# Twenty-one of the twenty-four unread matmuls in each of five RMSNorm waits are taken out of a two-layer diffusion backbone

## The chip, the cores and the metric

The kernel runs on one core of one Trainium2 chip. The metric is the device time of one execution in microseconds (us). A core has TensorE (matmuls), VectorE, ScalarE, GpSimd, and SyncE, which here issues DMAs.

## The reference

The program runs two layers over 256 latent tokens and 256 context tokens of width 1024, in fp32. Every layer is a half-step SwiGLU feed-forward, a token mixer (layer 0: a convolution module beside windowed attention; layer 1: a two-directional mLSTM), and a second half-step feed-forward. Each of these sub-layers begins with an RMSNorm, modulated by a conditioning vector, and the last layer is followed by one more.

```python
def rmsnorm(x, g):
    xf = x.astype(jnp.float32)
    y = xf * lax.rsqrt(jnp.mean(xf * xf, axis=-1, keepdims=True) + EPS)
    return (y * g.astype(jnp.float32)).astype(x.dtype)

def ffn_half(x, mods, g, w_gu, w_d):
    shift, scale, gate = mods
    h = modulate(rmsnorm(x, g), shift, scale) @ w_gu
    hg, hu = jnp.split(h, 2, axis=-1)
    return x + 0.5 * gate * ((jax.nn.silu(hg) * hu) @ w_d)
```

## The kernel before

All state is kept with the model width on the partitions: xT holds 8 tiles (KT = 8) of 128 partitions by 512 columns, the tokens of both streams. Seven norms are numbered 0 to 6. Norm 0 opens the first feed-forward (f0), norm 1 the even mixer (ev_in), norm 2 the feed-forward f1, norm 3 f2, norm 4 the odd mixer (od_gate, od_in), norm 5 f3 and norm 6 the output. Norms 0 to 4 run over 512 columns, norms 5 and 6 over 256, the latent tokens alone.

Weights come in units of 128 by 2048 numbers. For each, SyncE loads raw, ScalarE rounds it to w_hi (L936), and VectorE takes the difference as w_lo (L1241). Every product is three matmuls: high by high, low by high and high by low (L467 to L469). The buffers of raw, w_hi and w_lo are double, so unit u + 2 can be made only when TensorE is done with unit u. Activations are split in the same way into hn_hi and hn_lo.

A norm n passes through four engines, each of which works through its own list in order. Semaphores tie the lists together:

- ScalarE squares the tiles of xT as they are finished (L974), VectorE adds seven of them into acc (L1255).
- TensorE, in norm(n), waits for the last square and the last addition, and sums acc and the last square over the partitions against a column of ones, into one column for each block of 128 tokens (L524, L525).
- ScalarE takes the root (L946), and then makes w_hi of the unit LATE_UNIT[n], which it had put off for the norm. VectorE inverts (L1280), spreads the result on a diagonal (L1281), and makes w_lo of the same late unit.
- TensorE broadcasts the diagonal over all partitions with one fp32 matmul (L530).
- VectorE scales a tile into t_ring (L1297), ScalarE adds the shift and rounds to hn_hi (L952), and VectorE makes hn_lo (L1304) and raises hn_made. After each of the first tiles the first products of the next stage can begin: first_units takes five tiles of two units in turns (two tiles at 256 columns), 12 products for each tile.

In norms 1 to 5 TensorE also runs matmuls whose result nobody reads. keep_busy(n, count) first waits until the unit u = LATE_UNIT[n] - 1 is made and its bank is free, and then issues count matmuls of w_hi by w_hi, 512 columns each, into that bank (L516). The first real product of the stage overwrites it. norm(n) calls it three times: ahead of the wait for the squares, between the sums and the wait for the diagonal, and behind the broadcast. The table BUSY holds the three counts, 6, 7 and 11. Norms 0 and 6 have none.

Of the kernel before, what the change touches and what calls it, by code (L numbers as in the profile page):

```python
# [86 lines left out]
def build(nc, t, out):  # L87
# [3 lines left out]
    with ExitStack() as ctx:  # L91
# [216 lines left out]

        LATE_UNIT = {1: U["ev_in"] + 1, 2: U["f1upA"] + 1, 3: U["f2upA"] + 1, 4: U["od_in"], 5: U["f3upA"] + 1, 6: NU}
        ADDS = KT - 2  # L310
        BUSY = {n: (6, 7, 11) for n in range(1, 6)}

        STEP_TILE = ((2, 3, 0, 1), (3, 2, 1, 0))

# [148 lines left out]
        def _(pe):  # L463
# [46 lines left out]
            def keep_busy(n, count):  # L510

                u = LATE_UNIT[n] - 1
                pe.wait_ge(lo_made, u + 1)
                pe.wait_ge(unit_evac, u - 1)
                for _ in range(count):
                    pe.matmul(ps[:, bank(u, 1), :], w_hi[:, u % 2, 0:P], w_hi[:, u % 2, 0:TOK], start=True, stop=True)  # L516

            def norm(n):
                if n in BUSY:
                    keep_busy(n, BUSY[n][0])  # L520
                pe.wait_ge(sq_added, ADDS * (n + 1))
                pe.wait_ge(sq_made, KT * (n + 1))
                for i in range(W[n] // P):
                    pe.matmul(ps[:, 6, i:i + 1], acc[:, i * P:(i + 1) * P], ones[:, 0:1], start=True, stop=False)  # L524
                    last = pe.matmul(ps[:, 6, i:i + 1], sq[:, 1, i * P:(i + 1) * P], ones[:, 0:1], start=False, stop=True)  # L525
                last.then_inc(norm_mm, 1)
                if n in BUSY:
                    keep_busy(n, BUSY[n][1])
                pe.wait_ge(rstd_made, n + 1)
                pe.matmul(ps[:, 7, 0:W[n]], ones, rstd[:, 0:W[n]], start=True, stop=True).then_inc(rstd_mm, 1)  # L530
                if n in BUSY:
                    keep_busy(n, BUSY[n][2])

# [1335 lines left out]
```

## Time and profile before

| | us |
|---|---|
| median of 3 runs | 1868.83 |
| lowest and highest run | 1868.31, 1869.6 |
| the profiled execution | 1873.79 |
| span of its trace | 1871.9 |

| engine | busy us | share of the span |
|---|---|---|
| TensorE, matmuls | 1768.6 | 94% |
| TensorE, weight loads | 1483.5 | 79% |
| VectorE | 1161.2 | 62% |
| ScalarE | 622.2 | 33% |
| GpSimd | 68.4 | 4% |

The times of instructions below are those of the profiled execution. Records of matmuls overlap: one of 512 columns lasts 0.39 us in the trace while the next starts 0.23 us after it. So the pace of TensorE is read from starts and not from durations. The granted clock (PEclk) is 1.00 at 2.4 GHz and 0.50 at 1.2 GHz; its mean over the profiled execution is 0.973. A wait shows as idle time ahead of an instruction, in brackets, with what ended it.

### The profile page before, as it was taken

The page shows a single profiled execution, that of the slowest core. Times are in us where ns is not written, and L with a number is a line of the kernel's source. Part 1 is how long each engine was busy: PE and PEld are TensorE (multiplying, and loading weights), DVE is VectorE, ACT ScalarE, POOL GpSimd, SP SyncE. Part 2 cuts the span into 40 slices and gives each one's busy share as a digit, 9 for nine tenths or more (in the row PEclk, how much of TensorE's full clock was granted, in tenths as well). Part 3 has the DMA queues.
Part 4 walks back from the last instruction along what each step waited for, and adds up shares of the span by engine and source line. Part 5 has one row for each costly group of instructions (what it writes and reads, how often), then busy time and mean ns, then how long its engine had stood idle before and what let it go on. Part 6 is the DMA issues. An engine that isn't in the chain of part 4 may idle for free.

```text
span 1871.9 us, 23296 instructions
## 1 busy us (share of the span) xinstructions
PE 1768.6 (94%) x9187; PEld 1483.5 (79%) x9187; DVE 1161.2 (62%) x1765; ACT 622.2 (33%) x824; POOL 68.4 (4%) x133
## 2 busy tenths in 40 slices
PE   6899999999876999999999999999999999899997
PEld 4688888877543778888888788888887999899996
DVE  4477667875869557776778577533335536665454
ACT  3322223233564442312322332222224323454442
POOL 0011001100000000100100000000000000000000
PEclk9899999999986999999999999999999999999998
DMA  8455556552100125554556254232231222234543
GB/s 326 162 186 180 185 170 194 171 192 88 46 23 23 54 71 170 184 182 173 192 171 199 90 173 162 91 113 90 79 103 68 88 71 91 91 134 170 192 163 107
DMA packets 49041, 253.36 MB, mean 135 GB/s; under 512 B 5569, under 2 KB 7105, under 8 KB 32577
## 3 DMA queue, kind: packets, MB, share of 16 engines
q1 hardware_dynamic: 30384, 184.10, 28.4%
q0 software_dynamic: 18576, 68.17, 11.4%
q8 instruction: 54, 0.88, 0.2%
q14 instruction: 27, 0.21, 0.0%
HBM read 251.20 MB, written 1.05 MB: 135 GB/s over the span
## 4 chain that ended last, share of the span: by engine, by line
PE 86%; DVE 8%; ACT 4%; issue 1%; DMA 1%; SPq 0%; ACTq 0%; DVEq 0%
PE ps L467 27%; PE ps L468 27%; PE ps L469 27%; DVE y L1441 2%; DVE w_lo L1241 2%; ACT w_hi L936 1%; PE ps L804 1%; DVE t_ring L1297 1%; PE ps L833 1%; DVE hn_lo L1304 1%; ACT hn_hi L952 0%; PE ps L676 0%; PE ps L830 0%; PE ps L690 0%; DMA xT<-in_xT 0%
## 5 line engine op out<-in xcount | busy, mean ns | idle before, releaser
L467 PE MATMUL ps<-hn_hi,w_hi 128*128 128x512 f32 (+2 forms) x1784 | 649.3, 364 | 24.7 <-DVE hn_lo L1304 16.4
L468 PE MATMUL ps<-hn_lo,w_hi 128*128 128x512 f32 (+2 forms) x1784 | 641.2, 359 | 0.0
L469 PE MATMUL ps<-hn_hi,w_lo 128*128 128x512 f32 (+2 forms) x1784 | 641.1, 359 | 0.0
L1241 DVE TENSOR_TENSOR w_lo<-raw,w_hi 128x2048 fp32r<-128x2048 f32 (+2 forms) x184 | 377.0, 2049 | 345.5 <-ACT w_hi L936 345.3
L936 ACT ACTIVATE w_hi<-raw 128x2048 fp32r<-128x2048 f32 (+2 forms) x184 | 316.5, 1720 | 725.2 <-PE ps L469 725.2
L467 PEld LDWEIGHTS ps<-hn_hi,w_hi 128*128 128x128 f32 (+1 forms) x1784 | 339.5, 190 | 90.0 <-DVE hn_lo L1304 21.7
L469 PEld LDWEIGHTS ps<-hn_hi,w_lo 128*128 128x128 f32 (+1 forms) x1784 | 339.3, 190 | 50.6 <-issue 0.9
L468 PEld LDWEIGHTS ps<-hn_lo,w_hi 128*128 128x128 f32 (+1 forms) x1784 | 339.5, 190 | 48.5 <-issue 0.8
L467 PE MATMUL ps<-a_hi,w_hi 128*128 128x512 f32 (+1 forms) x704 | 255.4, 363 | 1.7 <-DVE a_lo L1371 1.7
L468 PE MATMUL ps<-a_lo,w_hi 128*128 128x512 f32 (+1 forms) x704 | 255.2, 362 | 0.0
L469 PE MATMUL ps<-a_hi,w_lo 128*128 128x512 f32 (+1 forms) x704 | 255.2, 362 | 0.0
L1345 DVE CUSTOM_DVE_ANT_0 t_ring<-mod_raw,cols 128x1024 f32<-128x1024 f32 x128 | 164.0, 1281 | 1.8
L1345 DVE CUSTOM_DVE_ANT_0 mod_raw<-mod_raw,cols 128x1024 f32<-128x1024 f32 x128 | 164.0, 1281 | 0.0
L467 PEld LDWEIGHTS ps<-a_hi,w_hi 128*128 128x128 f32 x704 | 132.9, 189 | 22.7 <-DVE a_lo L1371 2.1
L469 PEld LDWEIGHTS ps<-a_hi,w_lo 128*128 128x128 f32 x704 | 132.9, 189 | 20.6
L468 PEld LDWEIGHTS ps<-a_lo,w_hi 128*128 128x128 f32 x704 | 132.9, 189 | 20.5
L1260 DVE SCALAR_TENSOR_TENSOR xT<-ps,modT,xT 128x256 f32<-128x256 f32 x136 | 59.9, 480 | 133.2 <-PE ps L469 133.1
L992 ACT ACTIVATE a_hi<-prod 128x512 f32 (+3 forms) x88 | 50.9, 579 | 212.8 <-DVE prod L1368 212.8
L449 POOL DMA_DIRECT2D mod_raw<-in_mod_w x128 | 67.7, 529 | 1082.6 <-DVE modT L1345 1027.0
L1371 DVE TENSOR_TENSOR a_lo<-prod,a_hi 128x512 fp32r<-128x512 f32 (+1 forms) x88 | 55.1, 626 | 63.6 <-ACT a_hi L992 63.6
L1441 DVE SCALAR_TENSOR_TENSOR y<-upad,cols,y 128x512 f32<-128x512 f32 x120 | 81.2, 744 | 0.0
L467 PE MATMUL ps<-w_hi,hn_hi 128*128 128x256 f32 x256 | 76.4, 299 | 0.0
(201 smaller groups left out, 1253.3 us busy)
## 6 DMA issues: line engine op xcount, KB each, us to landing
raw<-in_w_up SPq DMA_DIRECT2D x88, 1024.0 KB, 4.9
mod_raw<-in_mod_w POOLq DMA_DIRECT2D x128, 512.0 KB, 3.8
raw<-in_w_downA SPq DMA_DIRECT2D x32, 768.0 KB, 4.2
raw<-in_w_downB SPq DMA_DIRECT2D x32, 640.0 KB, 3.9
raw<-in_w_od_in SPq DMA_DIRECT2D x16, 1024.0 KB, 4.9
mod_raw<-in_mod_first SPq DMA_DIRECT2D x8, 1024.0 KB, 7.6
raw<-in_w_ev_in SPq DMA_DIRECT2D x7, 1024.0 KB, 4.9
raw<-in_w_ev_out SPq DMA_DIRECT2D x4, 1024.0 KB, 5.0
```

Of the source, the lines that this page charges most:

```text
L449: pool.dma_start(mod_raw[:, q, :], t["mod_w"][i]).then_inc(mod_in[q], 16)
L467: pe.matmul(o, lh, rh, start=first, stop=False)
L468: pe.matmul(o, lh, rl, start=False, stop=False)
L469: return pe.matmul(o, ll, rh, start=False, stop=last)
L804: last = pe.matmul(ps[:, to + kt, 0:DH + 1], wk_ring[:, n % 2, kt * P:(kt + 1) * P], v_tok[:, STEP_TILE[d][s], h, :], start=True, stop=True)
L936: act.activation(w_hi[:, u0 % 2, 0:n], raw[:, u0 % 2, 0:n], ACT.Copy).then_inc(hi_made, 1)
L992: act.activation(a_hi[:, j + 2 * r, 0:w], prod[:, j, 0:w], ACT.Copy).then_inc(a_hi_made, 1)
L1241: dve.tensor_tensor(w_lo[:, u0 % 2, 0:n], raw[:, u0 % 2, 0:n], w_hi[:, u0 % 2, 0:n], ALU.subtract).then_inc(lo_made, 1)
L1260: last = dve.scalar_tensor_tensor(out=xT[:, d0 + 2 * r, tokens(s)], in0=ps[:, bank(u0, b), tokens(s)], scalar=modT[:, vec, d0 + 2 * r, s:s ...
L1345: last = dve.tensor_tensor_reduce(out=spent, in0=mod_raw[:, q, :], in1=c_row[:, s, :], scale=1.0, scalar=col("mod_b", m * KT + k), op0=ALU ...
L1371: dve.tensor_tensor(a_lo[:, j + 2 * r, 0:w], prod[:, j, 0:w], a_hi[:, j + 2 * r, 0:w], ALU.subtract).then_inc(a_made, 1)
L1441: ins = dve.scalar_tensor_tensor(out=dst, in0=src, scalar=col("conv_w", i * CT + c), in1=dst, op0=ALU.mult, op1=ALU.add)
```

## The change

One table changes. Of the 24 unread matmuls of each of the norms 1 to 5, the six ahead of the sums and the seven ahead of the broadcast go, and of the eleven behind the broadcast three stay: 3 in place of 24 in a norm, 15 in place of 120 in the kernel. The calls stay, and with them the two waits in each. All else is the same.

```diff
         ADDS = KT - 2
-        BUSY = {n: (6, 7, 11) for n in range(1, 6)}
+        BUSY = {n: (0, 0, 3) for n in range(1, 6)}
```

## Rows read from the trace of the kernel before

**Rows 1.** The page: busy us of TensorE, and lines of the chain that ended last.

```profile
PE 1768.6 (94%) x9187; PEld 1483.5 (79%) x9187; DVE 1161.2 (62%) x1765; ACT 622.2 (33%) x824; POOL 68.4 (4%) x133
...
PE ps L467 27%; PE ps L468 27%; PE ps L469 27%; DVE y L1441 2%; DVE w_lo L1241 2%; ACT w_hi L936 1%; PE ps L804 1%; DVE t_ring L1297 1%; PE ps L833 1%; DVE hn_lo L1304 1%; ACT hn_hi L952 0%; PE ps L676 0%; PE ps L830 0%; PE ps L690 0%; DMA xT<-in_xT 0%
```

**Rows 2.** Stretches, feed-forward f1: length, busy us (instructions) by engine, PEclk, DMA.

```profile
671.30:1031.60 360.30, 359.45 (x1584) 297.31 (x1585) 261.72 (x360) 98.64 (x102) 28.53 (x54) 1.00 0.52 171
```

**Rows 3.** Instructions in order of time, TensorE, norm 1: start, us, instruction, idle before.

```profile
411.56 1.52 PE L516 MATMUL ps<-w_hi 128*128 128x512 f32 x6
413.45 0.35 PE L524 MATMUL ps<-mats,acc 128*128 128x1 f32 x2 [0.37 <-ACT sq L974]
...
415.00 0.36 PE L525 MATMUL ps<-mats,sq 128*128 128x1 f32 x2
...
416.93 1.02 PE L530 MATMUL ps<-rstd,mats 128*128 128x512 f32 x2
417.38 3.07 PE L516 MATMUL ps<-w_hi 128*128 128x512 f32 x11
422.54 0.47 PE L467 MATMUL ps<-hn_hi,w_hi 128*128 128x512 f32 x1 [2.08 <-issue]
422.85 0.40 PE L468 MATMUL ps<-hn_lo,w_hi 128*128 128x512 f32 x1
423.08 0.39 PE L469 MATMUL ps<-hn_hi,w_lo 128*128 128x512 f32 x1
```

**Rows 4.** Instructions in order of time, VectorE, norm 1.

```profile
415.98 0.69 DVE L1281 TENSOR_TENSOR rstd<-mats,inv 128x512 f32<-128x512 f32 x1
417.50 2.29 DVE L1241 TENSOR_TENSOR w_lo<-raw,w_hi 128x2048 fp32r<-128x2048 f32 x1 [0.83 <-ACT w_hi L936]
419.71 1.65 DVE L1297 SCALAR_TENSOR_TENSOR t_ring<-xT,modT,ps 128x256 f32<-128x256 f32 x4
421.56 0.88 DVE L1304 SCALAR_TENSOR_TENSOR hn_lo<-t_ring,modT,hn_hi 128x256 fp32r<-128x256 f32 x2 [0.19 <-ACT hn_hi L952]
```

**Rows 5.** Instructions in order of time, TensorE, norms 2 and 3.

```profile
662.21 0.38 PE L524 MATMUL ps<-mats,acc 128*128 128x1 f32 x2 [1.78 <-DVE acc L1255]
...
667.01 1.32 PE L530 MATMUL ps<-rstd,mats 128*128 128x512 f32 x2
...
1033.49 0.35 PE L524 MATMUL ps<-mats,acc 128*128 128x1 f32 x2 [0.37 <-ACT sq L974]
...
1042.53 0.50 PE L467 MATMUL ps<-hn_hi,w_hi 128*128 128x512 f32 x1 [0.38 <-DVE hn_lo L1304]
```

**Rows 6.** Stretches inside norm 3.

```profile
1033.50:1035.30 1.80, 1.80 (x17) 1.80 (x17) 0.00 (x0) 1.15 (x1) 0.00 (x0) 1.00 0.62 259
...
1036.30:1039.60 3.30, 3.30 (x7) 1.99 (x6) 2.47 (x2) 1.21 (x1) 0.00 (x0) 0.50 0.00 0
```

**Rows 7.** Instructions in order of time, TensorE: products of 512 columns at the slow clock.

```profile
66.78 0.63 PE L468 MATMUL ps<-hn_lo,w_hi 128*128 128x512 f32 x1
67.21 0.63 PE L469 MATMUL ps<-hn_hi,w_lo 128*128 128x512 f32 x1
```

**Rows 8.** Stretches: dense work that begins slow, until the clock rises; one behind.

```profile
66.20:70.20 4.00, 4.00 (x10) 3.17 (x11) 0.00 (x0) 1.30 (x2) 0.00 (x0) 0.50 0.00 0
...
1538.70:1544.80 6.10, 6.10 (x20) 5.25 (x21) 1.51 (x4) 1.61 (x3) 0.00 (x0) 0.50 0.37 152
...
1628.70:1633.50 4.80, 4.80 (x23) 4.80 (x24) 4.34 (x7) 2.31 (x4) 0.00 (x0) 0.50 0.48 195
1633.60:1637.00 3.40, 3.40 (x30) 3.40 (x30) 0.00 (x0) 0.00 (x0) 0.00 (x0) 1.00 0.00 0
...
1418.90:1421.90 3.00, 2.97 (x12) 2.31 (x12) 2.96 (x8) 1.41 (x4) 0.00 (x0) 0.50 0.02 5
```

**Rows 9.** Instructions in order of time, TensorE: the sums of norm 0.

```profile
12.60 0.56 PE L524 MATMUL ps<-mats,acc 128*128 128x1 f32 x2 [12.60 <-DVE acc L1255]
13.01 0.57 PE L525 MATMUL ps<-mats,sq 128*128 128x1 f32 x2
```

## The prediction

> **What bounds the kernel now.** First the busy shares and the chain that ended last [rows 1]: TensorE is busy for 94% of the span, and the three product lines (L467 to L469) are 27% of the chain each, 81% together. Then the view of whole stages: in one feed-forward it is busy 359.45 of 360.30 us at the full clock [rows 2]. There every us that TensorE loses is a us of the kernel. Then the norm waits, where this does not hold, engine by engine. Norm 1 on TensorE [rows 3]: the last unit's products run until the six unread matmuls start at 411.56. The sums over partitions (L524, L525: 16 records, four one-column sums in two fp32 halves) start at 413.45, behind ScalarE's last square, and end near 415.23. Seven unread ones follow, the broadcast of 1/rms (L530) at 416.93, eleven unread ones from 417.38, then 2.08 us of nothing until the first product at 422.54. The other engines hold the chain [rows 4]: VectorE builds the diagonal (L1281) from 415.98 to 416.67, makes w_lo of the late weight unit from 417.50 to 419.79, and only then scales the first tile (419.71) and splits it (L1304, to 422.44). The first product starts 0.10 us behind that. So w_lo and the two steps behind it end last; the unread matmuls lie beside them.
>
> **What the removed matmuls cost now.** 21 in each of five norms go, 105 of 120. At full clock one takes 0.23 us, the distance of the products at 422.85 and 423.08 [rows 3]; that is 4.8 us of TensorE per norm, 24 us in all. None of it is on the chain. The six end before the sums can start (idle 0.37 us before them in norm 1, 1.78 us in norm 2 [rows 3, 5]). The seven stand ahead of the broadcast: it could start at about 416.7 and starts at 416.93, and its result isn't needed before w_lo is done at 419.79, so nothing is gained. The worst place is norm 2, where the seven ran at the slow clock and the broadcast ended at 667.01 + 1.32 = 668.33 [rows 5]. With w_lo at the same distance behind the sums as in norm 1 (419.79 - 413.45 = 6.34 behind their start) it is done at 668.55, so 0.2 us were left even then. Of the eleven the last ends 2.08 us before the first product in norm 1 and 0.38 us before it in norm 3 [rows 3, 5]. Direct gain: 0, and at most the 0.1 to 0.2 us a norm by which the seven could touch the broadcast; I take 0. The waits inside the helper (for lo_made and unit_evac) stay even with a count of 0; they were over long before and cost nothing. No queue gets a new wait, and no DMA moves.
>
> **What they cover.** The row to look at is the granted clock. In norm 3 TensorE had only one-column sums from 1033.50 to 1035.30; it counts as busy for 1.80 us, at clock 1.00, yet from 1036.3 to 1039.6 the granted clock is 0.50, that is 1.2 instead of 2.4 GHz, although the unread matmuls had begun again [rows 6]. Some 3.2 us after the last full-width work (the record of the six ends at 1033.49 - 0.37 = 1033.1 [rows 5]) the clock fell, and came back while the seven, the broadcast and the eleven kept the engine dense. Norm 2 shows it too (its broadcast lasts 1.32 us against 1.02 in norm 1 [rows 3, 5]). In both, the slow stretch fell wholly on unread work, and the real products started fast. That is the cover that goes. After the change TensorE has, between the last product (its record ends at about 411.7) and the first (422.5), only 16 one-column records, a broadcast of 0.9 us (two passes) and three matmuls of 0.7 us together, ending at 418.5, with 4 us of nothing behind them. I find no row with so thin a stretch that kept the clock. So the first products of norms 1, 2, 3 and 5 start at 1.2 GHz.
>
> **Price of a slow restart.** Products of 512 columns follow each other by 0.43 us at the slow clock (66.78 to 67.21 [rows 7]) and by 0.23 at the full one: of each slow us 1 - 0.227/0.427 = 0.47 us is lost. How long it lasts: dense work that began slow at 66.2, 1538.7, 1628.7 and 1418.9 stayed slow for 4.0, 6.1, 4.8 and 3.0 us [rows 8]; mean 4.5. Nothing in the rows says where in this spread a given norm will lie, so I take the mean, with 3.0 and 6.1 as bounds. Norms 1, 2 and 3: 3 x 4.5 x 0.47 = 6.3 us (bounds 4.2 and 8.6). Norm 5 has 256 columns: 4.8/23 = 0.209 us each slow against 3.4/30 = 0.113 fast [rows 8], a share of 0.46, so 2.1 us (1.4 to 2.8). VectorE makes a tile in 1.65/2 + 0.88 = 1.7 us [rows 4] and TensorE needs 12 products, 5.1 us slow and 2.7 fast, for it, so TensorE is the late one at once and the whole loss stays on the path. Norm 4 starts slow already: the sparse gate products run slowly, and the dense ones from 1418.9 stay slow for 3.0 us, the shortest of the four. There I take the mean again, 1.5 us more slow time, 0.7 us (0 to 1.5).
>
> The Trainium skill (TensorE: Matmul & The Clock Gate, section Terms) puts the penalty at throttled time x (1 - K/N), that is half of it; the rows give 0.47 at 512 columns. By that page of the Trainium skill the four restarts would cost 4 x 4.5 x 0.5 = 9.0 us in place of 8.4.
>
> **Price of slow sums.** The one-column sums are on the chain (ScalarE's root waits for the last). At full clock they take 1.78 us, 0.111 each; in norm 0, at the kernel's start, two pairs start 0.41 us apart, 0.21 each [rows 9], the slow pace whatever the clock column says there. All 16 slow would cost 1.6 us more. With the six gone, full-width work ends 1.4 us earlier (six at 0.23): 411.7 in norm 1, and 662.21 - 1.78 - 1.4 = 659.0 in norm 2 [rows 3, 5]. With norm 3's 3.2 us the clock falls at 414.9, so 0.3 us of sums are slow and cost 0.3 more, in norms 1, 3 and 4 alike; in norm 2 it falls at 662.2, as the sums start: 1.6. In norm 5 the eight sums come too soon: 0. Sum 2.5 us, bounds 0 and 6. The slow broadcast takes 1.7 us from about 416.9 and is still done at 418.6, ahead of w_lo: 0.
>
> The Trainium skill (TensorE: Matmul & The Clock Gate, Part 1, What's actually happening) ties the slow state to idle time. Norm 3 fell behind a stretch that the view counts as 1.80 us busy of 1.80, so the trace doesn't let busy sums count as cover. If only idle time counted, the sums would stay fast and the sum would be 2.5 us less, 1877.9; the restarts would stay slow, for 4 us idle are ahead of them.
>
> **Sum.** 6.3 + 2.1 + 0.7 + 2.5 = 11.6 us. The profiled execution took 1873.79 us (span 1871.9 and 1.9 around it), so it would take 1885.4. It lies 5.0 us over the median of the runs, 1868.83, by profiling and by its own slow stretches; on the median the same sum gives 1880.4, and that is the prediction (0.6% slower). The bounds add to 5.6 and 18.9 us: 1874.4 to 1887.7.
>
> **Rivals.**
> (A) The clock holds: the broadcast and three matmuls are cover enough, or the clock comes back before the first product. For it: in norm 1 an idle stretch of 2.08 us cost nothing, and broadcast and three matmuls at the slow clock are 3.0 us of dense work. Against it: 4 us idle follow instead of 2, and norm 3 lost the clock on less. Time 1868.8, chance 0.08.
> (B) Slow restarts, but partly given back, since the first units also wait for w_hi and w_lo of the next, or only norms 2, 3 pay: half of 8.4 us, 1873. Against it: stage occupancy 359.45 of 360.30. Chance 0.08.
> (C) Slow restarts at the long end and all sums slow: +19 us, 1888. Chance 0.09.
> (D) Faster. The unread matmuls themselves are late now: in norm 3 the slow clock left only 0.38 us before the first product [rows 5]. Should the clock fall a little earlier, inside the sums, the eleven at 0.43 instead of 0.23 us end 2.2 us later and push the first product by up to 1.8 us, in each of four norms: 7 us that the change would give back, 1862, if in turn the clock after it holds. It decides from the point where the seven, broadcast and eleven end later than the first hn_lo. Against it: no norm shows such a push, and it needs (A) too. Chance 0.03.
> The forecast itself, 1874.4 to 1886: 0.72.
>
> **Chances.** A difference of 0.2% (3.7 us) is about what this kernel's measurement can tell from none. Faster: (D) 0.03. Same: (A) and an eighth of (B), 0.09. Slower: 0.88. The range takes in most of (B) and the start of (C), 1872.8 to 1887.0, and leaves out about 0.2.
>
> **What would show it.** In the changed profile: granted clock 0.50 in the first 3 to 6 us after the first product of each of norms 1, 2, 3 and 5, with 0.43 us between them; the sums of norm 2 lasting about 3.4 us instead of 1.8; w_lo, t_ring and hn_lo at unchanged distances from the last sum; the feed-forward stages unchanged behind. Wrong if the first products are 0.23 apart (A), if TensorE idles later by less than before so that the stage ends on time (B), or if the first product comes closer to the last one before the norm than now (D).

## The result and the profile after

| | before | after |
|---|---|---|
| median us (6 runs each) | 1869.57 | 1877.94 |
| lowest and highest | 1868.31, 1873.51 | 1876.98, 1879.93 |
| span of the profile | 1871.9 | 1876.2 |
| mean granted clock | 0.973 | 0.962 |

The ratio is 1.004 with a 95% interval of 1.0027 to 1.0054: slower by 0.4%, that is 7.5 us, 5.0 to 10.1; the medians lie 8.4 us apart. In a later series on another occasion the same kernel gave 1.0046 (1.0033 to 1.0059).

The busy shares and the chain on the page of the changed kernel show nothing of it. TensorE is busy 14.3 us less than in [rows 1], its share of the span is the same, and the chain has the same head:

```profile
PE 1754.3 (94%) x9082; PEld 1470.1 (78%) x9082; DVE 1160.9 (62%) x1765; ACT 622.5 (33%) x824; POOL 68.7 (4%) x133
...
PE ps L467 27%; PE ps L469 27%; PE ps L468 27%; DVE y L1441 2%; DVE w_lo L1241 2%; ACT w_hi L936 1%; PE ps L804 1%; DVE t_ring L1297 1%; PE ps L833 1%; DVE hn_lo L1304 1%; PE ps L676 0%; ACT hn_hi L952 0%; PE ps L830 0%; PE ps L524 0%; PE ps L525 0%
```

One has to go to a norm. TensorE's instructions in order of time, norm 2 of the changed kernel (start, duration, instruction, idle before it and what ended that), to be held against [rows 3, 5]:

```profile
664.16 0.35 PE L524 MATMUL ps<-mats,acc 128*128 128x1 f32 x2 [3.34 <-DVE acc L1255]
...
667.59 2.05 PE L530 MATMUL ps<-rstd,mats 128*128 128x512 f32 x2 [1.45 <-DVE rstd L1281]
668.65 2.27 PE L516 MATMUL ps<-w_hi 128*128 128x512 f32 x3
...
673.26 0.80 PE L467 MATMUL ps<-hn_hi,w_hi 128*128 128x512 f32 x1 [2.34 <-DVE hn_lo L1304]
673.85 0.63 PE L468 MATMUL ps<-hn_lo,w_hi 128*128 128x512 f32 x1
674.28 0.63 PE L469 MATMUL ps<-hn_hi,w_lo 128*128 128x512 f32 x1
```

From the first sum to the first product it takes 9.10 us, as in norm 1 before (413.45 to 422.54, 9.09 [rows 3]) and within 0.03 us as in norm 2 before (9.07). So nothing was gained or lost within this norm. But the second and third product start 0.43 us apart. Stretches of the same kernel (length, busy us by engine, granted clock, DMA), each cut where the clock changes or a product begins:

```profile
417.10:420.10 3.00, 3.00 (x5) 1.45 (x5) 2.34 (x2) 0.63 (x1) 0.00 (x0) 0.50 0.41 169
420.20:422.70 2.50, 0.14 (x1) 0.00 (x0) 2.30 (x6) 1.70 (x4) 0.00 (x0) 1.00 0.66 174
422.80:423.50 0.70, 0.70 (x3) 0.61 (x4) 0.70 (x2) 0.00 (x0) 0.00 (x0) 1.00 0.99 421
423.60:426.90 3.30, 3.30 (x9) 2.61 (x8) 3.23 (x9) 1.82 (x4) 0.00 (x0) 0.50 0.16 67
...
673.30:676.10 2.80, 2.80 (x7) 2.24 (x8) 2.76 (x7) 1.16 (x3) 0.00 (x0) 0.50 0.56 237
676.20:679.00 2.80, 2.80 (x13) 2.29 (x13) 2.73 (x8) 1.47 (x4) 0.00 (x0) 1.00 0.00 0
1041.40:1044.70 3.30, 2.74 (x5) 1.00 (x3) 3.21 (x4) 0.16 (x2) 0.00 (x0) 0.50 0.00 0
1044.80:1046.40 1.60, 0.00 (x0) 0.00 (x0) 1.41 (x4) 1.51 (x4) 0.00 (x0) 1.00 0.94 236
1046.50:1050.50 4.00, 4.00 (x18) 3.29 (x19) 3.93 (x10) 1.82 (x4) 0.00 (x0) 1.00 0.39 164
...
1666.30:1669.30 3.00, 3.00 (x14) 3.00 (x15) 2.89 (x7) 1.52 (x3) 0.00 (x0) 0.50 0.77 314
```

Norm 2: slow for 2.9 us of products, 7 records in 2.8 us and then 13. Norm 5: slow for 3.2 us. Norm 1 is less plain: the broadcast and the three matmuls brought the clock back at 420.1, it was full when the first product began at 422.79, and fell at 423.5 for 3.4 us, behind the idle time. Norm 3 shows that a restart can escape: the clock came back at 1044.7, with nothing in flight any more, and stayed.

What this costs is read from the distance between the first product behind a norm and the first sum of the next, two starts that every profile has:

| stage, us | before | before, second profile | changed | changed, second profile |
|---|---|---|---|---|
| norm 1 to 2, even mixer | 239.67 | 236.68 | 241.37 | 241.50 |
| norm 2 to 3, f1 | 362.21 | 362.21 | 363.56 | 363.69 |
| norm 3 to 4, f2 | 362.26 | 362.25 | 362.21 | 364.68 |
| norm 4 to 5, odd mixer | 242.94 | 241.43 | 240.51 | 239.55 |
| norm 5 to 6, f3 | 194.56 | 194.56 | 195.94 | 197.27 |

The stages f1 and f2 are a good ruler: in all profiles of this document they took 362.07 to 362.29 us whenever their first product started at the full clock. f1 lost 1.35 us in the changed profile, which is 0.47 x 2.9. f3 is a weaker one. It took 194.56 us in both profiles of the kernel before, but 195.68 us with eleven unread matmuls behind the broadcast and none elsewhere, though no product of f3 was slow there: TensorE waited late in the stage for a w_lo. The mixers aren't such a ruler: they have slow stretches of their own, in all kernels, and differ by 3 us between two profiles of the kernel before.

### The profile page after: what moved, and what is told of

Same layout as the page of the kernel before. It is cut to its first block, busy times and chain, and to the rows that moved or that the text cites. A ratio compares the mean times of both kernels' runs of the same rounds, so it can differ in the third digit from the quotient of the medians.

```text
span 1876.2 us, 23086 instructions
## 1 busy us (share of the span) xinstructions
PE 1754.3 (94%) x9082; PEld 1470.1 (78%) x9082; DVE 1160.9 (62%) x1765; ACT 622.5 (33%) x824; POOL 68.7 (4%) x133
## 4 chain that ended last, share of the span: by engine, by line
PE 86%; DVE 8%; ACT 4%; issue 1%; DMA 1%; ACTq 0%; SPq 0%; DVEq 0%
PE ps L467 27%; PE ps L469 27%; PE ps L468 27%; DVE y L1441 2%; DVE w_lo L1241 2%; ACT w_hi L936 1%; PE ps L804 1%; DVE t_ring L1297 1%; PE ps L833 1%; DVE hn_lo L1304 1%; PE ps L676 0%; ACT hn_hi L952 0%; PE ps L830 0%; PE ps L524 0%; PE ps L525 0%
```

## The experiments

All were timed against the kernel before in five rounds. Where an entry shows no other edit, the kernel is the one before with another table. They fall into four series, in which the kernel before had medians of 1868.46 to 1869.61 us. Its runs lie mostly near 1868 or near 1873 us, so that a median can jump by some us: between kernels the ratios are to be compared, not the medians. All ratios and their intervals first:

| kernel, unread matmuls in a norm | median us | ratio to before | 95% interval |
|---|---|---|---|
| (12, 14, 22), 16 columns each | 1884.82 | 1.0084 | 1.0069 to 1.0099 |
| (0, 0, 0) | 1879.12 | 1.0049 | 1.0037 to 1.0061 |
| (0, 0, 3), the change | 1878.1 | 1.0046 | 1.0033 to 1.0059 |
| (0, 0, 3), held back | 1879.68 | 1.0050 | 1.0037 to 1.0063 |
| (6, 7, 3) | 1877.39 | 1.0038 | 1.0025 to 1.0052 |
| (0, 0, 3), in norm 4 (6, 7, 11) | 1879.28 | 1.0044 | 1.0028 to 1.0060 |
| (0, 0, 7) | 1872.4 | 1.0014 | 1.0004 to 1.0024 |
| (0, 0, 11) | 1870.96 | 1.0004 | 0.9995 to 1.0012 |
| (6, 7, 11), in norm 4 (0, 0, 3) | 1869.2 | 0.9999 | 0.9988 to 1.0011 |
| filled up to (7, 7, 19) | 1870.29 | 1.0012 | 1.0003 to 1.0022 |
| four more behind three gate products | 1871.83 | 1.0001 | 0.9989 to 1.0013 |
| (6, 7, 11), before once more | 1870.99 | 1.0004 | 0.9992 to 1.0017 |

**Is it the clock, or that TensorE is occupied?**

```diff
-        BUSY = {n: (6, 7, 11) for n in range(1, 6)}
+        BUSY = {n: (12, 14, 22) for n in range(1, 6)}
...
-                    pe.matmul(ps[:, bank(u, 1), :], w_hi[:, u % 2, 0:P], w_hi[:, u % 2, 0:TOK], start=True, stop=True)
+                    pe.matmul(ps[:, bank(u, 1), 0:16], w_hi[:, u % 2, 0:P], w_hi[:, u % 2, 0:16], start=True, stop=True)
```

> The kernel before with twice as many unread matmuls at the same three places (12, 14, 22), each with 16 moving columns in place of 512: their pace is that of the weight loads, 0.11 us in place of 0.23, so that TensorE stays busy for the same time in each norm, with almost nothing flowing through it. Theory 1 (the cover is full-width work, which keeps the granted clock): the clock falls in the norms as in the changed kernel, or more often, and the first products run 0.43 us apart: 7 to 13 us over the kernel before. Theory 2 (TensorE only has to be occupied, whatever flows): no loss, 0 to 1 us over the kernel before.

Measured: 1.0084, 15.7 us (12.9 to 18.5). Theory 2 is out, and the loss is above the 7 to 13 us that theory 1 gave. TensorE's instructions in order of time, norm 2:

```profile
658.79 1.40 PE L516 MATMUL ps<-w_hi 128*128 128x16 f32 x12
662.10 0.38 PE L524 MATMUL ps<-mats,acc 128*128 128x1 f32 x2 [1.90 <-DVE acc L1255]
...
664.19 3.13 PE L516 MATMUL ps<-w_hi 128*128 128x16 f32 x14
667.18 2.05 PE L530 MATMUL ps<-rstd,mats 128*128 128x512 f32 x2
668.24 5.48 PE L516 MATMUL ps<-w_hi 128*128 128x16 f32 x22
```

and its stretches:

```profile
662.10:663.60 1.50, 1.50 (x14) 1.50 (x14) 0.10 (x2) 1.04 (x1) 0.00 (x0) 1.00 0.00 0
663.70:673.50 9.80, 9.80 (x42) 8.77 (x41) 7.16 (x13) 4.32 (x8) 0.00 (x0) 0.50 0.34 109
673.60:677.20 3.60, 3.60 (x10) 2.83 (x11) 3.50 (x10) 2.02 (x5) 0.00 (x0) 0.50 0.00 0
```

From 663.7 to 673.5 TensorE is busy for 9.80 of 9.80 us and its clock is at half all the time, and for 3.7 us of products more. Here a busy share of 100% was no cover. The part of the loss that theory 1 had missed is there as well: at half clock each narrow matmul takes 0.21 us, the 22 end late, and the first product starts 673.58 - 662.10 = 11.48 us behind the first sum, against 9.07. Norms 1 to 4 take 2.1 to 2.4 us more each and norm 5 takes 2.8, 11.9 in all. The rest is slow products: f1, f2 and f3 take 1.7, 1.7 and 1.9 us more than before.

**Which of the three places carries it?** One edit of the table each: none at all; only the eleven; all but eight of the eleven.

```diff
-        BUSY = {n: (6, 7, 11) for n in range(1, 6)}
+        BUSY = {n: (0, 0, 0) for n in range(1, 6)}
```

> No unread matmul at all (0, 0, 0). Theory 1 (the three behind the broadcast still help: in the changed kernel the clock rose again at 1044.76, ahead of norm 3's first product): without them it comes back ahead of no first product, every restart of norms 1, 2, 3 and 5 is slow for 2 to 6 us, 9 to 13 us over the kernel before, so 2 to 5 us over the changed kernel. Theory 2 (the three are too few to matter): as the changed kernel, 7 to 8 us over the kernel before.

Measured: 1.0049 (1.0037 to 1.0061), 9.2 us; by the ratios that is 0.6 us over the changed kernel, less than the 2 to 5 us of theory 1. The intervals of the two overlap, so the time doesn't tell the theories apart. The profile is for theory 1: in none of the norms was the clock back ahead of the first product, and the stages f1, f2 and f3 lost 1.36, 2.25 and 3.52 us. The stretches behind the first products of norms 2, 3 and 5:

```profile
674.90:677.80 2.90, 2.81 (x7) 2.26 (x8) 2.87 (x8) 1.28 (x3) 0.00 (x0) 0.50 0.52 220
1048.40:1053.20 4.80, 4.80 (x11) 3.76 (x12) 4.73 (x12) 2.50 (x6) 0.00 (x0) 0.50 0.31 130
1668.60:1674.40 5.80, 5.80 (x27) 5.80 (x28) 5.44 (x13) 3.47 (x7) 0.00 (x0) 0.50 0.42 168
```

```diff
-        BUSY = {n: (6, 7, 11) for n in range(1, 6)}
+        BUSY = {n: (0, 0, 11) for n in range(1, 6)}
```

> Only the six and the seven are taken out (0, 0, 11). Theory 1 (what counts is the state of the clock at the first product, and the broadcast with the eleven, 1.1 + 4.7 us at the slow clock, brings it back in time): the clock falls in or behind the sums, rises before or soon after the first product, and only slow sums and a late first product cost something: 0.5 to 3 us over the kernel before. Theory 2 (the six and the seven are the cover): most of the loss of the changed kernel, 6 to 8 us over the kernel before.

Measured: 1.0004 (0.9995 to 1.0012), not to be told from the kernel before. Theory 2 is out: the six and the seven carry nothing that can be measured. Norm 2 of this profile is the worst case for them, in order of time on TensorE:

```profile
660.96 0.56 PE L524 MATMUL ps<-mats,acc 128*128 128x1 f32 x2 [3.34 <-DVE acc L1255]
...
663.94 0.57 PE L525 MATMUL ps<-mats,sq 128*128 128x1 f32 x2
665.96 2.04 PE L530 MATMUL ps<-rstd,mats 128*128 128x512 f32 x2 [1.45 <-DVE rstd L1281]
667.01 4.79 PE L516 MATMUL ps<-w_hi 128*128 128x512 f32 x11
671.63 0.48 PE L467 MATMUL ps<-hn_hi,w_hi 128*128 128x512 f32 x1
```

The stretches of the same norm:

```profile
660.40:670.50 10.10, 8.08 (x25) 6.44 (x26) 5.19 (x10) 4.20 (x6) 0.00 (x0) 0.50 0.06 10
670.60:671.60 1.00, 1.00 (x5) 0.63 (x4) 0.88 (x2) 0.85 (x3) 0.00 (x0) 1.00 0.72 262
```

The clock fell ahead of the sums, which ran 0.21 us apart and took 1.5 us more. It was back at 670.6, near the end of the eleven, and the first product started at full clock, f1 then taking 362.22 us. The whole price was 10.67 us in place of 9.07 in this one norm. Norms 1, 3 and 4 took 0.4 to 0.5 us more, with the slow eleven the last to end.

```diff
-        BUSY = {n: (6, 7, 11) for n in range(1, 6)}
+        BUSY = {n: (6, 7, 3) for n in range(1, 6)}
```

> Only eight of the eleven behind the broadcast are taken out (6, 7, 3). Theory 1: the clock holds through the sums, but about 4 us of nothing before the first product let it fall: slow restarts, 4 to 7 us over the kernel before, with the sums at full pace. Theory 2 (the six and the seven are the cover): 0 to 1 us over the kernel before.

Measured: 1.0038 (1.0025 to 1.0052), 7.1 us: theory 1. What taking out eight matmuls of each norm loses is not to be told from what taking out 21 does. Norm 3 of this profile is the case in its pure form, with the clock full through the sums and until 1041.0 (TensorE, in order of time):

```profile
1033.03 0.35 PE L524 MATMUL ps<-mats,acc 128*128 128x1 f32 x2 [0.37 <-ACT sq L974]
...
1036.50 1.02 PE L530 MATMUL ps<-rstd,mats 128*128 128x512 f32 x2
1036.96 1.26 PE L516 MATMUL ps<-w_hi 128*128 128x512 f32 x3
1042.07 0.79 PE L467 MATMUL ps<-hn_hi,w_hi 128*128 128x512 f32 x1 [3.84 <-DVE hn_lo L1304]
```

The stretch behind the first product:

```profile
1042.00:1047.80 5.80, 5.73 (x14) 4.47 (x15) 5.66 (x15) 2.73 (x6) 0.00 (x0) 0.50 0.29 123
```

It idles 3.84 us and restarts slow for 5.8 us; f2 takes 364.93 in place of 362.26 us, 2.7 more, which is 0.47 x 5.8. Norm 2 of the same profile shows the reverse side: there the seven ran at half clock and kept the broadcast until 666.05, 5.32 us behind the first sum. VectorE, done with w_lo, waited 0.52 us for it, and the first product came after 10.05 us in place of 9.07; slow sums account for most of the rest.

**How many behind the broadcast?**

```diff
-        BUSY = {n: (6, 7, 11) for n in range(1, 6)}
+        BUSY = {n: (0, 0, 7) for n in range(1, 6)}
```

> Seven unread matmuls behind the broadcast and none elsewhere (0, 0, 7). Theory 1 (the loss falls with the dense work behind the broadcast, steadily from 0 over 3 to 11): about halfway between the changed kernel and the one with eleven, 3 to 5 us over the kernel before. Theory 2 (what decides is whether the idle time before the first product is short enough, and seven leave some 3 us of it at the full clock but only 1.5 us at the slow one): 1 to 3 us over the kernel before.

Measured: 1.0014 (1.0004 to 1.0024), 2.6 us (0.8 to 4.5). It falls into the range of theory 2, and the interval reaches into that of theory 1. The step from three to seven gave back 6 us, that from seven to eleven 1.9: not a straight line, but this measurement can't show its shape. In its profile the clock was back ahead of the first product in norms 1, 2, 4 and 5, by 0.2 to 1.1 us, and only norm 3 restarted slow:

```profile
1036.92 3.97 PE L516 MATMUL ps<-w_hi 128*128 128x512 f32 x7
1041.53 0.80 PE L467 MATMUL ps<-hn_hi,w_hi 128*128 128x512 f32 x1 [0.64 <-DVE hn_lo L1304]
...
1041.50:1045.30 3.80, 3.77 (x9) 3.00 (x10) 3.72 (x9) 1.82 (x4) 0.00 (x0) 0.50 0.43 179
```

The idle time ahead of the first product was 0.64 us in norm 2 as well, which restarted at the full clock. So the length of that idle time alone, on which theory 2 rests, doesn't decide.

**Does it matter when the three run?** They wait for VectorE's first scaled tile:

```diff
+                    pe.wait_ge(t_made, KT * n + 1)
                     keep_busy(n, BUSY[n][2])
```

> The changed kernel (0, 0, 3), with the three matmuls held back until VectorE has scaled the first tile, some 2 us ahead of the first product, in place of right behind the broadcast. Theory 1 (the sooner dense work is seen before the first product, the earlier the clock is back behind it; the place of the three matters): 1 to 3 us less than the changed kernel, 4 to 7 us over the kernel before. Theory 2 (only the amount of work in the norm matters): as the changed kernel, 7 to 8.5 us over the kernel before.

Measured: 1.0050 (1.0037 to 1.0063). Theory 1 missed: nothing came back. In its profile norms 1, 2, 3 and 5 restarted slow for 4.8, 2.7, 1.6 and 2.5 us, a mean of 2.9. In norms 1 to 4 the clock was down ahead of the broadcast, and norms 1, 3 and 4 took 9.81, 9.70 and 10.34 us in place of 9.09, 9.04 and 9.13. Moving the three by these 2 us gained nothing.

**Is the loss the same in each run?**

> The changed kernel (0, 0, 3) once more, beside the others on the same chip, for a second profile. Theory 1 (the place of the slow stretches within a norm is by chance, their sum over the norms is not): again 7 to 8.5 us over the kernel before, with the slow time at other norms than in the first profile. Theory 2 (each norm has its fixed loss): the same norms slow, for the same times, as in the first profile.

Measured: 1.0046. Its profile is the second one in the table of stages. The products behind norms 1, 2, 3 and 5 were slow for 3.4, 2.9, 0 and 3.2 us in the first profile, and for 3.4, 3.1, 5.2 and 6.2 us in the second; norm 3 went from nothing to 2.42 us of loss. That is theory 1 for norms 3 and 5: they have no fixed loss. The other half of theory 1, that the sum over the norms is fixed, failed: the slow time is 9.5 us in the first profile and 17.9 in the second. The spans are equal all the same (1876.2 and 1876.3), because the start and f0, the odd mixer, the norms 4 and 5 and the end were shorter in the second. Norms 1 and 2 lost the same both times, and two profiles can't say whether that is chance.

**Norm 4, and the profile of before.** The odd mixer's stage was shorter in the changed kernel. Two tables share the change out:

```diff
-        BUSY = {n: (6, 7, 11) for n in range(1, 6)}
+        BUSY = {n: (0, 0, 3) if n == 4 else (6, 7, 11) for n in range(1, 6)}
```

> The change in norm 4 alone: (0, 0, 3) there, (6, 7, 11) in norms 1, 2, 3 and 5. Theory 1 (in norm 4 the change gains: the clock has then fallen before the sparse gate products and is back 3.5 to 5.4 us behind the first of them, where in the kernel before it falls 1.2 us behind it and is back after 8 to 9 us): the gate transposes (L778) come 18.6 to 18.7 us behind the first product instead of 19.9 to 20.4, less up to 0.5 us for slow sums, so 0 to 1.5 us less than the kernel before. Theory 2 (the prediction's: norm 4 loses 0.7 us and its sums 0.3): 1 us over the kernel before, and the transposes no earlier.

```diff
-        BUSY = {n: (6, 7, 11) for n in range(1, 6)}
+        BUSY = {n: (6, 7, 11) if n == 4 else (0, 0, 3) for n in range(1, 6)}
```

> The change in norms 1, 2, 3 and 5 alone: (0, 0, 3) there, (6, 7, 11) in norm 4. Theory 1: these four carry more than the whole loss, 8 to 10 us over the kernel before, some 1 us over the changed kernel. Theory 2: 6.5 to 7.5 us over the kernel before, 1 us less than the changed kernel.

Measured: 0.9999 (0.9988 to 1.0011) and 1.0044 (1.0028 to 1.0060), 8.2 us. Norm 4 carries nothing that can be measured; the other four carry the loss. Whether they carry 1 us more or less than the whole can't be said from this interval. For norm 4 both theories failed in the profile. With (0, 0, 3) in norm 4 the gate transposes came 19.91 us behind the first product, as in the kernel before (19.94, and 20.42 in its second profile). With (6, 7, 11) there and the change elsewhere they came after 18.57, as in the changed kernel (18.72 and 18.59). So the 1.3 us hang not on what stands in norm 4, but on whether the clock falls among the sparse gate products. The other profiles agree: the transposes came after 19.55 to 20.42 us in the five in which the clock fell 0.3 to 2.3 us behind the first gate product, and after 17.5 to 18.7 us in the nine in which it had fallen before or didn't fall there. What makes it fall there in one kernel and not in the other stays open.

> The kernel before once more, for a second profile beside the others. Theory 1 (the profile on which the prediction rested was itself late by slow stretches in layer 1's mixer, 242.94 us from the first product behind norm 4 to the sums of norm 5, where seven profiles of other variants have 238.4 to 240.5): a span of 1866 to 1869 us, that stage some 239 us, with the first products of norms 1, 2, 3 and 5 again at the full clock. Theory 2 (the stage is that long in this kernel): 242 to 243 us again.

Measured: median 1870.99, ratio 1.0004 to the runs beside it; the profile's span is 1867.9, inside theory 1's range. Norms 1 to 5 took 9.09, 9.07, 9.04, 9.13 and 6.99 us and the feed-forwards 362.21, 362.25 and 194.56: restarts at full clock, as expected. The odd mixer took 241.43 us, between the two theories. The 4.0 us between the two profiles lie in the two mixers, 3.0 and 1.5 us, less 0.5 us for the start and f0. For the even mixer slow time doesn't explain it: the longer stage had a mean granted clock of 0.89, the shorter one 0.88. What makes the 3.0 us isn't shown.

**Can the cover be made better?** The gate products of norm 4 got four unread matmuls each for the first three; another kernel also filled what was idle in all norms (7, 7, 19 in norms 1, 3 and 4; 13, 7, 19 in norm 2; 8, 7, 15 in norm 5).

```diff
+                    if k < BEHIND:
+                        for _ in range(4):
+                            pe.matmul(ps[:, bank(u, 1), :], w_hi[:, u % 2, 0:P], w_hi[:, u % 2, 0:TOK],
+                                      start=True, stop=True)
                 if step >= BEHIND:
```

> The kernel before with four more unread matmuls behind each of the first three gate products of norm 4, where VectorE sets the pace and the clock fell in the profile of before. Theory 1 (one more slow restart is covered and nothing is pushed): 1 to 2 us less than the kernel before. Theory 2 (the clock falls elsewhere all the same, or the matmuls are late at the slow clock, four at 0.43 us on top of 1.3 us of products in 1.7 us): 0 to 2 us over the kernel before.

> The opposite of the change: the idle stretches that the kernel before still has are filled too. Counts (7, 7, 19) in norms 1, 3 and 4, (13, 7, 19) in norm 2, (8, 7, 15) in norm 5, and four unread matmuls behind each of the first three gate products of norm 4. Theory 1 (the last slow restart, norm 4's, and the slow sums go): 1 to 3 us less than the kernel before. Theory 2 (the unread matmuls are then themselves late where the clock still falls in the sums, which they don't cover: nineteen at 0.43 us are 8.1 us): 0 to 4 us over the kernel before.

Measured: 1.0001 (0.9989 to 1.0013) for the gate alone, and 1.0012 (1.0003 to 1.0022) for all of it. Neither beats the kernel before. The matmuls among the gate products halved the slow stretch there, 3.4 us in place of 6.8, but the transposes came after 19.99 us, no earlier than before. In the filled kernel the clock still fell behind the sums, and then the matmuls themselves were late, norm 3:

```profile
1031.83 2.85 PE L516 MATMUL ps<-w_hi 128*128 128x512 f32 x7
1034.48 1.68 PE L530 MATMUL ps<-rstd,mats 128*128 128x512 f32 x2
1035.40 5.08 PE L516 MATMUL ps<-w_hi 128*128 128x512 f32 x19
1040.32 0.39 PE L467 MATMUL ps<-hn_hi,w_hi 128*128 128x512 f32 x1
```

The first product stands directly behind the nineteen, 10.27 us behind the first sum in place of 9.04. Three norms lost 1.2 us each in this way. That is mechanism (D) of the prediction, in a kernel that has more of these matmuls.

## Why the prediction was right

The time, 1877.94, lies in the range, and the sign and the main mechanism hold. The sum came out too high: 11.6 us against 7.5 by the ratio and 8.4 by the medians.

- **Direct gain 0: right.** In the changed profile norm 2 takes 9.10 us and norm 1 9.08, with 21 matmuls less in each. The experiment (0, 0, 11) adds that 13 of the 21 could go without a measurable loss. That the seven never hold up the broadcast, even at the slow clock, was off by a little: in (6, 7, 3) norm 2 waited 0.52 us for it.
- **Slow restarts: the right term, mis-sized.** The mean of eight restarts in two profiles of the changed kernel is (3.4 + 2.9 + 0 + 3.2 + 3.4 + 3.1 + 5.2 + 6.2)/8 = 3.4 us, where the prediction took 4.5. Times 0.47 that is 1.6 us a norm, 6.4 in all in place of 8.4. The price of a slow us was right: 2.9 us cost 1.35 in f1, 5.2 us cost 2.42 in f2. The 6.4 us are slow time at this price; for norm 1, whose products open a mixer, the loss itself can't be read.
- **The step that failed** is the one from "I find no row with so thin a stretch that kept the clock" to slow first products in all of norms 1, 2, 3 and 5. It left out that the clock, once down, can come back ahead of the first product. The broadcast and the three, put at 3.0 us of dense work and 1.06 + 1.28 = 2.3 us by their starts, were followed by a full clock ahead of norm 1's first product in both profiles, which only moved the slow stretch to 0.7 and 1.0 us behind it, and ahead of norm 3's in the first, which saved it whole. Of eight first products three started at the full clock. Without the three (0, 0, 0) none did. So rival (A), given 0.08 for all norms together, came true in a single norm of one profile. The spread of 3.0 to 6.1 us had been read from places where the clock was down when the dense work began; it had no room for a restart of 0.
- **Slow sums: the right mechanism, mis-sized.** Predicted 2.5 us, 1.6 of it in norm 2. In the first changed profile the sums cost nothing in norms 1 and 2, and the norms 3, 4 and 5 were 0.62, 0.46 and 0.44 us longer, 1.5 in all; in the second only norm 3 was, by 0.55. Norm 5 had been put at nothing. The clock fell in norm 2 at 665.9, as the last sum ran, not as they began. The 3.2 us between the last full-width work and the fall, carried over from norm 3 of the kernel before, were no constant: in the norms 1 to 5 of the first changed profile it was 2.4 to 5.1 us. That it can fall ahead of them is shown by (0, 0, 11), where norm 2 paid 1.6 us.
- **Norm 4, +0.7 us: wrong in sign for the profiles, nothing in the runs** (0.9999). The stage was shorter by 0.9 to 3.4 us in the changed profiles than in those of before, and the experiments didn't tie that to the counts in norm 4.
- **The profiled execution as a base.** The sum against 1873.79 gave 1885.4, but the profile took 1878.01. The prediction had put the 5.0 us over the median down to profiling and slow stretches. The second profiled execution of before took 1869.73, and runs of that kernel reach 1874.7, so the 5.0 us lie within its own spread and nothing points at profiling. The two profiles differ chiefly in the mixers, and that slow stretches make this difference isn't shown.
- **The rule on idle time**, which the prediction weighs against its own, would have taken the sums out, 1877.9, which is close to the measured time. That is luck: the narrow matmuls lost the clock with TensorE busy 9.80 of 9.80 us, and sums did run slow in norms 3 to 5. The Trainium skill's 0.5 in TensorE: Matmul & The Clock Gate, section Terms, against 0.47 makes 0.4 us here and isn't resolved.

Of the mean loss, 6.4 us of restarts and (1.5 + 0.55)/2 = 1.0 of sums are read from two profiles, 7.4 together against 7.5 measured. The agreement is in part luck. Two profiles of stretches that vary by 6 us are thin ground for it, and it leaves the mixers out: in the mean of the two profiles on either side the even mixer was 3.3 us longer in the changed kernel, 1.6 of which the sum has as norm 1's restart, and the odd mixer 2.2 us shorter.

## What to carry to other kernels

Work that nobody reads may be what keeps TensorE's clock up, and its place decides: the matmuls that run last, up to the restart, carry all of it that can be measured here, and those ahead of them carried nothing measurable. Judge such cover by the granted clock and the distance between the first products behind a wait, never by the busy share. Too much of it can do harm too, since it is slow itself just when the clock is down; and a single profile of a kernel with such stretches is a sample of one.

## What the runs showed of the hardware that was not expected

- TensorE at 100% busy with matmuls of 16 columns stood at half clock for 9.8 us, and went on so for 3.7 us of full-width products (673.6 to 677.3).
- The clock rose at 1044.7 with no matmul in flight any more, and fell at 423.5 in the midst of dense products, 0.7 us after their start. In both places the clock changed against what the engine was doing just then, so the clock of a product hangs on what was done ahead of it.
- A slow restart of dense 512-column products lasted between 0 and 6.2 us at the same places of the same kernel in two executions, 0 to 2.7 us of loss each time.
- The same kernel spreads over 6.7 us (the kernel before, 1867.2 to 1873.9 in 23 runs of one series), and two of its profiles differ by 4.0 us, chiefly in the two mixers. The even mixer was 3.0 us shorter in the profile in which it had the lower granted clock, 0.88 against 0.89.
